# Second layer of a two-block kernel: value tiles loaded between stores, recurrent steps reordered, gate product moved beside the attention

## The chip, the cores and the metric

The kernel runs on one core of one Trainium2 chip. The metric is the device time of one execution in microseconds (us). TensorE (PE) multiplies matrices; VectorE (DVE), ScalarE (ACT) and GpSimd (POOL) do the elementwise work; SyncE (SP) issues nearly all DMA transfers, in the order of its program. Each engine runs its own instructions in order and waits for others on semaphores.

## The reference

A first block (spatial gating, a state space mixer, a router with 16 experts) is followed by a second one, which the change concerns. With 1024 tokens and width 1024:

```python
def hybrid_layer(x, c, ...):
    h = rms_norm_2(x, g_pre) * (1 + scale) + shift
    q, k, v, g_att, u, g_lru, merge = jnp.split(h @ w_in, split_at, axis=-1)
    y_a = (dilated_attention(q, k, v) * jax.nn.silu(g_att)) @ w_pa
    u = causal_depthwise_conv(u, conv_w, conv_b)          # four taps
    y_b = (rg_lru(u, ...) * jax.nn.silu(g_lru)) @ w_pb
    gate_a, gate_b = jnp.split(jax.nn.sigmoid(merge), 2, axis=-1)
    return x + gate * rms_norm_2((gate_a * y_a + gate_b * y_b) @ w_o, g_post)

def rg_lru(u, ...):
    r, i = sigmoid(u @ w_rg + b_rg), sigmoid(u @ w_ig + b_ig)   # block diagonal
    log_a = -LRU_C * r * softplus(-lru_lambda)
    xin = sqrt(-expm1(2 * log_a)) * (i * u)
    h_t = exp(log_a)_t * h_{t-1} + xin_t                        # a scan over the tokens
```

The attention has 12 heads, in three groups of four with dilations 1, 4 and 16.

## The kernel before

Every large product is made in three passes over high and low parts (`three_passes`, L1351 to L1353): an operand is rounded to fp32r on ACT or POOL (the high part), and the rest is subtracted on DVE or POOL (the low part).

**Values.** The second layer starts by turning the normalised tokens and multiplying them with the value weights, 12 tiles of the weight stream (`I_ATT` to `I_PAIR`), in three groups of four tiles. A tile goes into one of four slots of `ring`; SP loads it when PE has finished with the tile before it in the slot, POOL splits it (L1169 high, L1172 low), and PE needs the split tile. Meanwhile ACT scales the eight row tiles of the first layer's result (L2299), and SP stores them (L1022).

**Products in pairs.** All other input products are 30 `PAIRS` p, each made of 7 smaller products i = 0..6 (12 matmuls each, `product(p, i)`), whose sums are put together by ACT (i = 0 at L2359, i = 4 at L2375) and DVE (i = 1, 2, 3, 5, 6 at L3157, L3160, L3175). A product waits for the sums that empty its bank or that it accumulates on: i = 5 for the sum of i = 2, i = 6 for that of i = 3, i = 2 of the next pair for that of i = 5, i = 3 of the next for that of i = 6. The weights of pair p+1 are split by ACT (L2326, at i = 3 to 6 of pair p) and POOL (L1273). A pair that makes gates is followed by `("act", p)`, a Silu or Sigmoid on ACT (L2385), and `("spill", p)`, two stores to DRAM (`gd`).

**The order by hand.** `ORDER2` is one list of events that every engine walks through. In its first part, 84 products (12 pairs), the eight recurrent channels c are woven in: channel c starts behind product `CHANNEL_AT[c]` with `conv` (four taps on DVE, L3184, L3186 twice, L3187, into the one buffer `uc`); three products later comes `gate` (four plain fp32 matmuls of `uc` on PE, L1821; on ACT four sigmoids L2393 and L2395, a Tanh L2400 and an Exp L2401); at +7 `gated` on DVE (L3192, L3194, L3195), at +8 `root` (Sqrt on ACT, L2405), and at +10 `scan` (L3200, L3201), whose result goes to DRAM (`hsd`). The next channel starts at +8 (once at +9).

**Attention units.** Then come six units u of two heads: the pairs Q and K, and a third pair whose products fill the gaps of the attention. For each of eight token tiles tt there are `S` (scores, PE L1831, softmax maximum on DVE), `E` (Exp on ACT, L2411), `PT` (turning, PE L1842, copied by ACT at L2420) and `O` (times V, PE L1854, copied at L2425). With tile 5 and later the first products of the next unit's Q are put in. In the last unit these places hold `B0`, the first half tile of the product of the recurrent branch with `w_pb`. Its operand y is made there: SP reloads the scans and the Silu gates (`yl_raw`, `yl_there`, 16 transfers of 512 KB), POOL multiplies them (L1289), ACT makes the high part (L2429) and DVE the low part (L3222), in the events `("y", c)`.

**The end.** `TURN_ORDER` mixes the rest of the recurrent branch (`B`) with the turning of the combined attention (`OT`, PE L1877), whose three groups DVE combines (L3255 to L3259); then come the other branch (`A`) and the output product.

## Time and profile before

| quantity | value |
|---|---|
| median of 3 runs | 2843.64 us (2843.12 to 2843.66) |
| the profiled execution's own time | 2843.31 us |
| its span in the trace | 2841.5 us |
| TensorE busy | 2736.1 us, 96% of the span |
| VectorE, ScalarE, GpSimd busy | 66%, 53%, 37% |

Terms of the sum are lengths in the profiled execution. Its own time is 1.8 us longer than its span and 0.3 us below the median. The second layer is the part behind about 1700 us. In the rows a time is in us from the span's start; `x8` counts instructions; square brackets hold the idle time of the engine just before and what released it. Starts and lengths of neighbouring matmuls overlap in the record: matmuls of 0.39 us follow each other every 0.23 us.

### The profile page before, as it was taken

What the parts mean: (1) busy time and instruction counts of PE and PEld (TensorE: products, weight loads), DVE (VectorE), ACT (ScalarE), POOL (GpSimd) and SP (SyncE); (2) the same over time, 40 slices, a digit from 0 to 9 for tenths busy, and PEclk for the clock granted to TensorE, in tenths of its full rate; (3) what the DMA queues carried; (4) which work ended last, traced back from release to release, by engine and by line L of the source; (5) the groups of instructions that cost most, each with busy time, mean ns of one, the idle gap of its engine ahead of it and who ended that gap; (6) DMA issues with size and microseconds to landing.
All of it is one profiled execution on the core that took longest, in us unless ns stands there. A gap on an engine that the chain in (4) does not pass through costs nothing.

```text
span 2841.5 us, 35547 instructions
## 1 busy us (share of the span) xinstructions
PE 2736.1 (96%) x12846; PEld 2237.8 (79%) x12846; DVE 1869.3 (66%) x1991; ACT 1495.7 (53%) x1854; POOL 1053.3 (37%) x510
## 2 busy tenths in 40 slices
PE   7999999999999999999999998998899999997999
PEld 6887888478888888888888877986678888886787
DVE  8972114888888888888888887327773233336663
ACT  4231013477777777777777765145564444443021
POOL 0012232013222233333332223567877555555530
PEclk9999999999999999999999999999999999998999
DMA  5021114599999999999999964122222222228441
GB/s 165 30 68 37 38 60 157 236 398 392 383 383 382 383 382 377 388 383 383 382 383 380 379 231 173 54 102 80 86 85 95 84 87 90 76 90 289 142 178 60
DMA packets 162779, 607.41 MB, mean 214 GB/s; under 512 B 20545, under 2 KB 47185, under 8 KB 129649
## 3 DMA queue, kind: packets, MB, share of 16 engines
q1 hardware_dynamic: 156912, 584.84, 54.4%
q0 software_dynamic: 5328, 20.07, 2.5%
q8 instruction: 68, 1.11, 0.2%
q10 hardware_dynamic: 434, 1.08, 0.1%
q14 instruction: 37, 0.30, 0.0%
HBM read 547.11 MB, written 57.78 MB: 213 GB/s over the span
## 4 chain that ended last, share of the span: by engine, by line
PE 81%; DVE 13%; ACT 2%; issue 2%; DMA 1%; POOL 1%; SPq 0%; DVEq 0%; ACTq 0%; POOLq 0%
PE bank L1685 23%; PE bank L1351 17%; PE bank L1353 16%; PE bank L1352 16%; PE bank L1698 2%; PE bank L1821 1%; DVE buffer L3186 1%; PE bank L1831 1%; PE bank L1854 1%; DMA buffer<-gd 1%; POOL buffer L1289 1%; DVE buffer L3187 1%; DVE buffer L3255 1%; PE bank L1842 0%; DVE buffer L3195 0%
## 5 line engine op out<-in xcount | busy, mean ns | idle before, releaser
L2949 DVE TENSOR_TENSOR slots_lo<-buffer,slots_hi 128x2048 fp32r<-128x2048 f32 x383 | 849.2, 2286 | 101.7 <-ACT slots_hi L2194 101.7
L2194 ACT ACTIVATE slots_hi<-buffer 128x2048 fp32r<-128x2048 f32 x384 | 708.8, 1951 | 40.8 <-PE bank L1685 25.4
L1232 POOL DMA_INDIRECT xacc<-buffer x15 | 276.5, 18430 | 615.6 <-ACT buffer L2262 615.6
L1273 POOL TENSOR_TENSOR w_lo_set<-buffer,w_hi 128x512 fp32r<-128x512 f32 x210 | 306.6, 1493 | 155.3 <-ACT w_hi L2326 153.9
L1685 PE MATMUL bank<-slots_hi,xsT_hi 128*128 128x512 f32 x960 | 257.8, 390 | 3.4 <-DVE xsT_lo L2967 3.4
L1685 PE MATMUL bank<-slots_lo,xsT_hi 128*128 128x512 f32 x960 | 257.4, 390 | 0.0
L1685 PE MATMUL bank<-slots_hi,xsT_lo 128*128 128x512 f32 x960 | 257.4, 390 | 0.0
L1685 PEld LDWEIGHTS bank<-slots_hi,xsT_hi 128*128 128x128 f32 x960 | 180.9, 189 | 41.2 <-issue 3.6
L1685 PEld LDWEIGHTS bank<-slots_lo,xsT_hi 128*128 128x128 f32 x960 | 180.8, 188 | 37.7
L1685 PEld LDWEIGHTS bank<-slots_hi,xsT_lo 128*128 128x128 f32 x960 | 180.8, 188 | 37.6
L1351 PE MATMUL bank<-slots_hi,heT_hi 128*128 128x512 f32 x512 | 202.5, 396 | 3.1 <-DVE heT_lo L2999 3.1
L1353 PE MATMUL bank<-slots_hi,heT_lo 128*128 128x512 f32 x512 | 199.6, 390 | 0.0
L1352 PE MATMUL bank<-slots_lo,heT_hi 128*128 128x512 f32 x512 | 199.4, 389 | 0.0
L1351 PE MATMUL bank<-t_hi,w_hi 128*128 128x512 f32 x480 | 194.9, 406 | 0.0
L1353 PE MATMUL bank<-t_hi,w_lo_set 128*128 128x512 f32 x480 | 188.9, 393 | 0.0
L1352 PE MATMUL bank<-t_lo,w_hi 128*128 128x512 f32 x480 | 188.7, 393 | 0.0
L3175 DVE TENSOR_TENSOR buffer<-bank,buffer 128x512 f32<-128x512 f32 x90 | 72.1, 802 | 175.3 <-PE bank L1353 174.6
L2326 ACT ACTIVATE w_hi<-buffer 128x512 fp32r<-128x512 f32 x210 | 120.2, 623 | 100.5 <-POOL buffer L1265 82.8
L1351 PE MATMUL bank<-hT_hi,w_hi 128*128 128x512 f32 x360 | 145.1, 403 | 0.0
L1353 PE MATMUL bank<-hT_hi,w_lo_set 128*128 128x512 f32 x360 | 140.7, 391 | 0.0
L1352 PE MATMUL bank<-hT_lo,w_hi 128*128 128x512 f32 x360 | 140.7, 391 | 0.0
L2021 ACT ACTIVATE buffer<-bank,buffer 128x512 f32<-128x512 f32 x32 | 22.1, 690 | 194.9 <-PE bank L1353 194.9
(538 smaller groups left out, 5661.5 us busy)
## 6 DMA issues: line engine op xcount, KB each, us to landing
buffer<-in_w_gate SPq DMA_DIRECT2D x128, 1024.0 KB, 7.8
buffer<-in_w_up SPq DMA_DIRECT2D x128, 1024.0 KB, 4.8
buffer<-in_w_down SPq DMA_DIRECT2D x128, 1024.0 KB, 7.8
buffer<-in_wstream SPq DMA_DIRECT2D x154, 512.0 KB, 4.2
gd<-buffer SPq DMA_DIRECT2D x28, 512.0 KB, 3.8
buffer<-gd SPq DMA_DIRECT2D x28, 512.0 KB, 7.6
buffer<-in_x SPq DMA_DIRECT2D x16, 512.0 KB, 8.3
od<-buffer SPq DMA_DIRECT2D x48, 130.0 KB, 1.8
```

What stands on the lines that cost most here:

```text
L1232: nc.gpsimd.indirect_dma_start(out=xacc, out_offset=bass.IndirectOffsetOnAxis(ap=idx_scatter, axis=0), in_=ys, in_offset=None, compute_op= ...
L1273: nc.gpsimd.tensor_tensor(lo, chunk_raw[p % 2][i], hi.bitcast(F32), ALU.subtract).then_inc(chunk_split.sem, 1)
L1289: nc.gpsimd.tensor_tensor(yl_raw(c), yl_raw(c), halves(yl_there[:, c]), ALU.mult).then_inc(yl_made.sem, 1)
L1351: mm(bank, lhs[0], rhs[0], start=first, stop=False, skip_group_check=goes_on)
L1352: mm(bank, lhs[0], rhs[1], start=False, stop=False, skip_group_check=goes_on)
L1353: return mm(bank, lhs[1], rhs[0], start=False, stop=last, skip_group_check=goes_on)
L1685: last = mm(psum[first_bank + c][:], x[:, k, :], w_[:, c * HALF:(c + 1) * HALF], start=(k == 0 and x is xsT_hi and w_ is w[0]), stop=(k == ...
L1698: last = mm(psum[4 + c][:], x[:, KD - 1, :], w_[:, c * HALF:(c + 1) * HALF], start=False, stop=x is xsT_lo)
L2194: fn(slots_hi[:, n_ % NH, :], slots[n_ % NS], ACT.Copy).then_inc(slot_high_ready, 1)
L2326: fn(w_hi[n_ % 8], chunk_raw[p % 2][i], ACT.Copy).then_inc(chunk_high.sem, 1)
L2949: tt2(slots_lo[:, place_of(n_), :], slots[n_ % NS], slots_hi[:, n_ % NH, :].bitcast(F32), ALU.subtract).then_inc(slot_split, 1)
L3175: tt2(dst, y_, x_, ALU.add).then_inc(post_done.sem, 1)
```

## The change

Four things, all in the second layer.

1. The loads of value tiles 4 and 5 are issued between the stores of the rows, and tiles 6 and 7 ahead of the first pair's weights.
2. In the recurrent channels the first tap of `conv` goes from DVE to ACT (an Identity with scale and bias, 128x1024), and the square of the decay (L3194) from DVE to ACT. `gate` comes 5 products behind `conv` instead of 3, a new step `mix` (the multiplication of L3192, and ACT's square) at +7, `gated` with what is left of it at +8, `root` at +9, `scan` at +10. Where two fall on one place, the later step of the older channel comes first; before, `conv` did.
3. y is made in 16 pieces of 128x512 during the units: SP loads the scan and the gate (2 x 256 KB), DVE multiplies (`ymul`), SP stores to a new DRAM tensor `yld`. Three pieces fall into each of five units, the last into the sixth. The last unit only loads y. POOL makes the low parts of channels 4 to 7 and DVE those of 0 to 3; `B0` holds two times two channels instead of two times four, and the other four go to the start of `TURN_ORDER`.
4. In the units, one more product of the next Q lies inside the attention, and `act` and `spill` of the fill pair come three products later, so behind the last `E`; in the last unit they come at the very end.

```diff
-CHANNEL_STEPS = (("conv", 0), ("gate", 3), ("gated", 7), ("root", 8), ("scan", 10))
+CHANNEL_STEPS = (("conv", 0), ("gate", 5), ("mix", 7), ("gated", 8), ("root", 9), ("scan", 10))
...
     events = [("prod", p, i)]
-    if i == 0 and p - 1 in GATE_PAIRS:
+    fill = p > N_LRU_PAIRS
+    if i == 3 * fill and p - 1 in GATE_PAIRS:
         events.append(("act", p - 1))
-    if i == 2 and p - 1 in GATE_PAIRS:
+    if i == 2 + 3 * fill and p - 1 in GATE_PAIRS:
         events.append(("spill", p - 1))
+    u, name = (p - N_LRU_PAIRS) // 3, PAIRS[p][0]
+    if name in "QK" or p >= N_LRU_PAIRS:
+        for j, (load, store) in enumerate((((1, 0), (1, 2)), ((1, 4), (1, 6)), ((2, 0), (2, 2)))):
+            if 3 * u + j < 16:
+                if ((p - N_LRU_PAIRS) % 3, i) == load:
+                    events.append(("yload", 3 * u + j))
+                if ((p - N_LRU_PAIRS) % 3, i) == store:
+                    events.append(("ymul", 3 * u + j))
...
-    events += product_events(q, 0) + [("S", u, 0)] + product_events(q, 1) + [("E", u, 0), ("S", u, 1)]
+    events += product_events(q, 0) + [("S", u, 0)] + product_events(q, 1) + [("S", u, 1), ("E", u, 0)]
+    ahead = 2 if last else 3
+    if not last:
+        events += product_events(q, 2)
...
-            events += [("y", c) for c in {1: (4,), 2: (5,), 3: (6, 7), 4: (0, 1), 5: (2, 3)}.get(tt, ())]
+            events += [("y", c) for c in {2: (4,), 3: (5, 6), 4: (7,), 5: (0, 1), 6: (2, 3)}.get(tt, ())]
+    if last:
+        events += [("act", q), ("spill", q)]
...
-TURN_ORDER = [("B", 0, 1), ("B", 1, 0), ("B", 1, 1)]
+TURN_ORDER = [("B", 0, 0), ("B", 0, 1), ("B", 1, 0), ("B", 1, 1)]
...
+                elif kind == "yload":
+                    j = event[1]
+                    c, ts_ = j // 2, slice((j % 2) * HALF, (j % 2 + 1) * HALF)
+                    u = j // 3
+                    hs_stored.wait(sp, 16 * 8)
+                    if j:
+                        y_stored.wait(sp, 16 * j)
+                    for i in range(2):
+                        gates_stored[i].wait(sp, 32 * stores_before(N_LRU_PAIRS + 3 * u + (u + i) % 2))
+                    sp.dma_start(temps[u % 2][:, 1], hsd[c][:, ts_]).then_inc(y_loaded.sem, 16)
+                    sp.dma_start(temps[1 - u % 2][:, 1], gd[GATE_ROW["lg"] + c][:, ts_]).then_inc(y_loaded.sem, 16)
+                elif kind == "ymul":
+                    j = event[1]
+                    yl_made.wait(sp, j + 1)
+                    sp.dma_start(yld[j // 2][:, (j % 2) * HALF:(j % 2 + 1) * HALF], temps[j // 3 % 2][:, 1]).then_inc(
+                        y_stored.sem, 16)
...
-                    fn(ra, ra, ACT.Exp, scale=lru_s[:, c:c + 1]).then_inc(act_to_lru, 1)
+                    fn(ra, ra, ACT.Exp, scale=lru_s[:, c:c + 1]).then_inc(decay_made.sem, 1)
+                elif kind == "mix":
+                    decay_made.wait(act, event[1] + 1)
+                    ii_done.wait(act, event[1] + 1)
+                    fn(uc, ra, ACT.Square).then_inc(act_to_lru, 1)
+                elif kind == "conv":
...
+                    if c:
+                        act.wait_ge(lru_to_act, c)
...
+                    fn(uc, ubufs[c % 2][:, 3:3 + SEQ], ACT.Identity, scale=tap(0, c), bias=col("conv_b", c)).then_inc(
+                        tap_done.sem, 1)
...
-                    step(ts(uc, x[:, 3:3 + SEQ], tap(0, c), col("conv_b", c), ALU.mult, ALU.add))
...
-                    step(tt2(uc, ra, ra, ALU.mult))
                     stt(th, uc, 1.0, th, ALU.add, ALU.mult).then_inc(lru_to_act, 1)
```

SyncE at the first value group, before and then after: `xfd` holds the rows, the single tiles of `in_wstream` at L851 and L865 are value tiles, the twos at L992 and L1006 the first pair's weights.

```order
L988 DMA vd<-buffer 128x512 x4
L1022 DMA xfd<-buffer 128x1024 x8
L992 DMA buffer<-in_wstream 128x1024 x2
L851 DMA buffer<-in_wstream 128x1024 x4
L988 DMA vd<-buffer 128x512 x4
```

```order
L1002 DMA vd<-buffer 128x512 x4
L1035 DMA xfd<-buffer 128x1024 x2
L865 DMA buffer<-in_wstream 128x1024
L1035 DMA xfd<-buffer 128x1024 x2
L865 DMA buffer<-in_wstream 128x1024
L1035 DMA xfd<-buffer 128x1024 x4
L865 DMA buffer<-in_wstream 128x1024 x2
L1006 DMA buffer<-in_wstream 128x1024 x2
```

Two value tiles moved between the rows, and the weights behind all four.

VectorE in the recurrent part, one channel's end and the next one's taps, before (L3192 to L3195 `gated`, L3184 to L3187 `conv`, L3200 and L3201 `scan`) and then after (L3234 `mix`, L3238 `gated`, L3229 and L3230 `conv`, L3244 and L3245 `scan`).

```order
L3192 TENSOR_TENSOR buffer<-buffer 128x1024
L3194 TENSOR_TENSOR buffer<-buffer 128x1024
L3195 SCALAR_TENSOR_TENSOR buffer<-buffer 128x1024
L3175 TENSOR_TENSOR buffer<-bank,buffer 128x512 x2
L3184 TENSOR_SCALAR buffer<-buffer 128x1024
L3186 SCALAR_TENSOR_TENSOR buffer<-buffer 128x1024 x2
L3187 SCALAR_TENSOR_TENSOR buffer<-buffer 128x1024
L3200 TENSOR_TENSOR buffer<-buffer 128x1024
L3201 SCALAR_TENSOR_TENSOR buffer<-buffer 128x1024
```

```order
L3234 TENSOR_TENSOR buffer<-buffer 128x1024
L3203 TENSOR_TENSOR buffer<-bank,buffer 128x512
L3238 SCALAR_TENSOR_TENSOR buffer<-buffer 128x1024
L3229 SCALAR_TENSOR_TENSOR buffer<-buffer 128x1024 x2
L3230 SCALAR_TENSOR_TENSOR buffer<-buffer 128x1024
L3220 TENSOR_TENSOR buffer<-bank,buffer 128x512
L3244 TENSOR_TENSOR buffer<-buffer 128x1024
L3245 SCALAR_TENSOR_TENSOR buffer<-buffer 128x1024
```

Two instructions of the chain left VectorE, and a sum (L3203) stands between the pieces of the older channel.

ScalarE near the end of an attention unit, before (L2385 the fill pair's activation, L2411 `E`, L2425 and L2420 the copies of `O` and `PT`) and then after (L2416, L2457, L2471, L2466).

```order
L2385 ACT_TABLE_LOAD
L2385 ACTIVATE buffer<-buffer 128x2x512 x2
L2425 ACTIVATE buffer<-bank 128x256
L2420 ACTIVATE buffer<-bank 128x256
L2411 ACT_TABLE_LOAD
L2411 ACTIVATE buffer<-buffer 128x128 x2
```

```order
L2457 ACTIVATE buffer<-buffer 128x128 x2
L2471 ACTIVATE buffer<-bank 128x256
L2466 ACTIVATE buffer<-bank 128x256
L2357 ACTIVATE w_hi<-buffer 128x512 x2
L2416 ACT_TABLE_LOAD
L2416 ACTIVATE buffer<-buffer 128x2x512 x2
L2471 ACTIVATE buffer<-bank 128x256
```

The activation, and with it both switches of the table, moved from between two `E` to behind the last `PT`.

## Rows read from the trace of the kernel before

**Rows 1.** The page: busy time, share of the span and instructions of each engine.
```profile
PE 2736.1 (96%) x12846; PEld 2237.8 (79%) x12846; DVE 1869.3 (66%) x1991; ACT 1495.7 (53%) x1854; POOL 1053.3 (37%) x510
```

**Rows 2.** PE's waits, 1700 to 2842: waiting, releaser, us in total, times, longest.
```profile
PE bank L1821 <- DVE buffer L3187: 22.4, 7, 4.7
PE bank L1854 <- ACT buffer L2420: 19.5, 10, 8.2
PE bank L1351 <- POOL ring_lo L1172: 10.1, 1, 10.1
PE bank L1842 <- ACT buffer L2411: 8.8, 6, 1.7
```

**Rows 3.** Chain of waits, 1725 to 1765: start, length, what.
```profile
1734.74 8.33 ACT buffer L2299 x8
...
1746.33 6.60 DMA buffer<-in_wstream
...
1752.98 3.17 POOL ring_hi L1169
...
1756.22 4.27 POOL ring_lo L1172
```

**Rows 4.** Timeline of PE, and windows: PE, PEld, DVE, ACT, POOL busy, clock, DMA.
```profile
1760.54 0.81 PE L1351 MATMUL bank<-ring_hi,hT_hi 128*128 128x512 f32 x1 [10.12 <-POOL ring_lo L1172]
...
1760.00:1765.00 5.00, 4.46 (x13) 3.84 (x14) 4.96 (x2) 1.91 (x1) 4.92 (x3) 0.62 0.42 140
...
1895.00:2135.00 240.00, 217.57 (x854) 162.77 (x854) 172.88 (x117) 141.05 (x181) 188.47 (x100) 0.96 0.22 83
2150.00:2550.00 400.00, 388.80 (x1911) 327.58 (x1910) 127.22 (x203) 174.89 (x409) 232.80 (x184) 0.99 0.25 85
2555.00:2612.00 57.00, 39.70 (x188) 32.47 (x187) 38.38 (x38) 25.21 (x61) 38.18 (x17) 0.85 0.81 287
```

**Rows 5.** Timeline of PE in the recurrent part: gate matmuls without and with a wait.
```profile
1900.49 3.59 PE L1821 MATMUL bank<-buffer 128*128 128x512 f32 x8
...
1988.52 5.40 PE L1821 MATMUL bank<-buffer 128*128 128x512 f32 x8 [4.62 <-DVE buffer L3187]
```

**Rows 6.** Timelines of DVE and ACT in the recurrent part.
```profile
1870.77 0.69 DVE L3175 TENSOR_TENSOR buffer<-bank,buffer 128x512 f32<-128x512 f32 x1 [4.68 <-PE bank L1353]
1873.49 0.69 DVE L3175 TENSOR_TENSOR buffer<-bank,buffer 128x512 f32<-128x512 f32 x1 [2.03 <-PE bank L1353]
...
1895.17 2.61 DVE L3186 SCALAR_TENSOR_TENSOR buffer<-buffer 128x1024 f32<-128x1024 f32 x2
...
2005.68 1.58 DVE L3192 TENSOR_TENSOR buffer<-buffer 128x1024 f32<-128x1024 f32 x1
2007.30 2.20 DVE L3194 TENSOR_TENSOR buffer<-buffer 128x1024 f32<-128x1024 f32 x1
...
2021.45 3.24 DVE L3201 TENSOR_TENSOR_SCAN buffer<-buffer 128x1024 f32<-128x1024 f32 x1
...
1905.34 1.15 ACT L2400 ACTIVATE buffer<-buffer 128x1024 f32<-128x1024 f32 x1
```

**Rows 7.** Timeline of ACT late in unit 4, and what PE waited for there.
```profile
2514.55 1.28 ACT L2385 ACT_TABLE_LOAD   x1
2515.85 2.01 ACT L2385 ACTIVATE buffer<-buffer 128x1024 f32<-128x1024 f32 x2
...
2520.64 0.44 PE L1842 MATMUL bank<-buffer 128*128 128x128 f32 x2 [1.48 <-ACT buffer L2411]
```

**Rows 8.** Timelines of POOL, ACT and PE in the last unit.
```profile
2574.16 2.34 POOL L1289 TENSOR_TENSOR buffer<-buffer 128x1024 f32<-128x1024 f32 x1 [16.25 <-DMA buffer<-gd]
...
2576.53 1.06 ACT L2429 ACTIVATE yl_hi<-buffer 128x1024 fp32r<-128x1024 f32 x1 [6.24 <-POOL buffer L1289]
...
2600.18 1.22 PE L1854 MATMUL bank<-buffer 128*128 128x128 f32 x4 [8.20 <-ACT buffer L2420]
```

**Rows 9.** The page's DMA issues: how many, KB each, median us to landing.
```profile
gd<-buffer SPq DMA_DIRECT2D x28, 512.0 KB, 3.8
buffer<-gd SPq DMA_DIRECT2D x28, 512.0 KB, 7.6
```

122 lines of the change are left out of this document (66 added, 56 removed).

## Prediction

> **What bounds the kernel now.** I read the page first: TensorE is busy 96% of the span [rows 1], so nothing but its 4% of pauses, and the stretches at the lower clock, can be won; no matmul is added or removed. Then its table of waits in the second layer [rows 2]. The four longest make 60.8 us, and the change goes for all of them: the gate matmuls wait 22.4 us for the last tap of the convolution, the attention's O waits 19.5 us and its PT 8.8 us for ScalarE, and the second value group waits 10.1 us for one split weight tile. Third, the windows, for what the clock takes on top [rows 4]: in 1895 to 2135 the granted clock is 0.96 of full, so 240 x 0.04 = 9.6 us more; in 1760 to 1765 it is 0.62, 5 x 0.38 = 1.9 us; in 2150 to 2550 it is 0.99, 4 us. The two levels are 2.4 and 1.2 GHz, and the same eight gate matmuls take 3.59 us without a wait and 5.40 us behind one of 4.62 us [rows 5]: a pause of about 4 us costs 1.8 us again. So some 61 us of waits and 16 us of clock are there to be had, and the question is how much of it the new order gives back.
>
> **Value tiles.** PE's wait is 10.12 us [rows 4], so group 0 ended at 1760.54 - 10.12 = 1750.4. The chain is ScalarE's eight row tiles, 8.33 us from 1734.74 (1.04 each), the stores and the weights in SP's order, the tile's load landing 6.60 us after its issue (1746.33), and 3.17 + 4.27 us of GpSimd [rows 3]. After the change the load goes out behind the second row, at about 1734.7 + 2 x 1.04 + 1 of issue + 1 for the load = 1738.8; it lands by 1745.4 with the same 6.6 us and is split by 1752.8 with the same contended 7.4 us. But VectorE is what GpSimd shares that time with, and it starts its joins only when all rows are stored (it did at 1748.3, between the load and the split); so most of the split meets an idle VectorE. With less traffic ahead, I take 1750 and no wait, and 1750.4 to 1755.3 as the range (landing 9 us, full contention). The gain is 10.1 + 1.9 = **12.0 us**, at worst 7. Two loads among the rows delay the last row by about 2.7 us, hence the joins; the first pair needs them some 60 us later, which covers that. Nothing else moves: tiles 5 to 7 are there sooner than PE, at 11 us a tile, wants them.
>
> **Recurrent channels.** Unit of time: one product, 2.72 us (two sums that each follow a product stand 2.72 us apart, 0.69 us long) [rows 6]. A 128x1024 step on VectorE costs 1.3 us alone (2.61 for two) and 2.20 us beside GpSimd [rows 6]. GpSimd is busy 188 of 240 us here [rows 4], so I take 2.2 for taps and `gated`, 1.6 for the multiplication, 1.15 for a 1024-wide ACT step, and 1.6 + 3.24 for `scan`. Let 0 be the end of the product at +6, so `mix` comes first. VectorE: a sum to 0.7, `mix` to 2.3. ScalarE squares to 3.4. VectorE: sum of the next product (ends at 2.7) to 3.5, `gated` to 5.7. ScalarE's tap to 6.9. VectorE's three taps to 13.5. The gate now stands behind five further products, at 6 x 2.72 = 16.3, so **its wait is gone** (22.4 us). What is late next: the sums of those products, which stand in VectorE's queue behind the taps. PE runs into them where product i = 5 or 6 comes three behind an unsummed one, or i = 2 or 3 four behind.
>
> Place by place, with i the first product behind `conv`. Channel 1 (i = 1): ScalarE has a Silu in the way (a table load 1.28 and 2.01 [rows 7]), the tap ends at 8.5, the taps at 15.2, the sums of i = 1 and 2 at 16.6; i = 5 wanted them at 13.6: stop 3.0. Channel 2 (i = 2): taps 13.6, sum 14.3, i = 5 wanted it at 10.9: 3.4. Channel 3 (i = 3): a Silu between Exp and square, sum at 15.2, wanted at 10.9: 4.3. Channel 4 (i = 4): none. Channel 5: 0.7. Channel 6: none. Channel 7 (i = 1, with a Sigmoid): 3.0. Together **14.4 us of new stops**, on PE's product waits instead of its gate waits. The scan behind the taps (4.8 us, to about 20) meets the gate and its 3 us on PE, and costs nothing as long as the taps are no later. Clock: four stops of 3 to 4.3 us against five of 3.5 to 4.7 us, 6.6 against 9.6 us. Result 32.0 - 21.0 = **11 us**. Bounds: taps at 1.3 us (GpSimd idle) shorten every stop by 2.7 us, leaving 2.9 us and no clock loss, a gain of 29; each of the four stops 2 us longer (a ScalarE that is late with the tap) leaves a gain of 1. I take the contended end, since the steps of rows 6 in mid channel are at 2.20.
>
> A table switch shows as 1.28 us, and the activation starts right behind it, 2515.85 after 2514.55 [rows 7]. The Trainium skill, "ScalarE: Activation LUTs", section "What ACT_TABLE_LOAD costs", adds a drain of 1.38 us to each switch. This trace has no such gap at that row. By the page three of the stops would be 1.4 us longer and the sum 4 us smaller. Another rule speaks against steps beside GpSimd. The rows show 2.20 us beside it against 1.3 us alone for one shape [rows 6]. "SBUF — State Buffer" in the Trainium skill, section "SBUF: two separate sides", calls the port that both share an exclusive lock: a step waits out a whole GpSimd instruction, then runs at full speed. By that, with 2.34 us of GpSimd [rows 8] ahead of every tap, three taps would take 10.9 us, and the first rival below would be the outcome; no step of these rows is that long, so it adds little to that rival's chance.
>
> **Attention units.** The activation of the fill pair takes 1.28 + 2.01 us, and then Exp's own table 1.28 us, all between two E's; PT waits 1.48 us behind it in unit 4 [rows 7]. The five units carry 11.2 of the 28.3 us of [rows 2] (the window 2150 to 2550 has 400 - 388.8 us idle [rows 4]) and 4 us of clock. Now both switches stand behind the last PT. What waits for them: O's copy, which nothing on PE needs, and the next unit's first E, which has two products, 5.4 us, above it for a softmax of about 1 us, a table of 1.28 and the Exp. So **15 us**, at worst 9 if the new DVE multiplications hold up the softmax. Those are 16 steps of about 0.7 to 1.2 us on an engine busy 127 of 400 us [rows 4], with 768 KB each of traffic in a window with the DMA queues at a quarter. Their loads have two products of 2.72 us to land. Where they are late, VectorE stands up to 2 us with two sums queued behind, inside the 5.4 us that those have. SP stands in front of each store; queued behind it are O's stores, the value loads (three tiles ahead) and, once per unit, none of the pair weights, which are issued first.
>
> **Last unit.** PE idles 57 - 39.7 = 17.3 us in 2555 to 2612 [rows 4], mostly in 4.6 and 8.2 us where ScalarE's copy of PT stands behind a high part that waits for GpSimd, which waits for reads of 512 KB, 16 of them in all (idle 16.25 us, then 2.34 us and 1.06 us each) [rows 8]. About 6.8 us of matmuls run at the low clock there, 2.5 us lost. After: eight of the sixteen 512 KB reads and all multiplications are gone, the high parts start behind tile 2, with four products (15 us) above the load. But tiles 5 to 7 have no product between PT and O, only 1.4 us of B0: there each copy waits for 2 x 1.06 us of high parts. I count 0.5 + 0.8 + 1.0 + 0.7 + 1.2 us for PT and O of these tiles, and 1.0 us where the low parts of channels 2 and 3 come late: 5.2 us, and a clock drop at most. The activation at the very end holds SP's statistics back by 1.28 + 2.01 us and two stores; 2.7 us of B that moved behind O cover it. So 17.3 + 2.5 - 5.2 - 1.8, rounded down for that tail: **12 us**, 5 to 17.
>
> **Sum.** 12 + 11 + 15 + 12 = 50 us. The profiled execution took 2843.3 us, so 2793.3; the median of the runs is 0.3 us above it. Forecast **2793 us**. Half of the forecast's uncertainty is the recurrent part.
>
> **Rivals.**
> - *VectorE's debt eats the recurrent gain.* Stops at sums as long as the old gate waits: the other three parts alone, 2843 - 39 = 2804. For it: VectorE's chain per channel loses only 2 steps of about 3 us, and ScalarE gets two more with waits in its queue; against it: the gate's slack is 13.6 us instead of 8.2.
> - *Everything hides.* With two steps fewer, GpSimd and VectorE meet less, taps near 1.3 us: recurrent 29 instead of 11, last unit 17: 2843 - 73 = 2770.
> - *The value tile isn't earlier.* Traffic of the rows delays the load as before, and 7 to 12 us stay: about 2802.
> - *Slower: SP blocks.* Each piece of y is a round trip in SP's queue: 7.6 us for the read, 0.7 for the step and 3.8 us for the store [rows 9] make 12 us against 5.4 us of cover, and if it reached PE each time, 16 x 6.7 = 107 us, 2843 - 50 + 107 = 2900. It turns the sign from 3.1 us per piece on. Against it: those landings are of 512 KB, the pieces are half, and the queues are idle then.
>
> **How the numbers follow.** Forecast 0.5, VectorE's debt 0.2, value tile 0.08, everything hides 0.17, slower 0.03, and 0.02 for no change. The range 2776 to 2812 takes in the forecast with its bounds and the first and third rival, and leaves out most of "everything hides" and the slow one. A difference of 0.2% (5.7 us) is what a measurement of this kernel tells from none. Faster 0.95, same 0.02, slower 0.03.
>
> **What would show it.** PE's wait for `ring_lo` gone; waits for L3187's successor small, and new ones of 3 to 4 us at L1351 on a DVE sum, in channels 1, 2, 3 and 7; the PT waits of units 0 to 4 gone; in the last unit waits of about 1 us at tiles 5 to 7. Wrong would be: a gate wait above 2 us, a wait on `w_lo_set` (GpSimd or ScalarE late with weights), or waits on VectorE's multiplication of y.

## The result and the profile after

The changed kernel takes **2791.3 us** (median of four runs, 2789.5 to 2793.9) against 2843.4 us before (median of four, 2839.1 to 2843.7). The ratio is 0.982, with a 95% interval of 0.980 to 0.984. The forecast was 2793 us. Its profiled execution took 2791.3 us, with a span of 2789.5 us.

To see where the 52.0 us between the two spans went, I cut both traces at the same five events of the program. Each row below is the time from one event to the next, read from the timelines; the code of the first and the last stretch is unchanged.

| stretch | before | after | saved | forecast |
|---|---|---|---|---|
| start to the first product of the value group 0 (1697.64, 1694.44) | 1697.6 | 1694.4 | 3.2 | 0 |
| values: to the first sum of pair 0 (1859.89, 1844.70) | 162.2 | 150.3 | 12.0 | 12 |
| recurrent: to S(0,0) (2184.94, 2162.52) | 325.1 | 317.8 | 7.2 | 11 |
| units: to S(5,0) (2558.37, 2517.82) | 373.4 | 355.3 | 18.1 | 15 |
| last unit: to the first OT (2628.83, 2576.78) | 70.5 | 59.0 | 11.5 | 12 |
| from there to the end | 212.7 | 212.7 | 0.0 | 0 |

The first row is no work of the change. Over the kernels of this study, all with the same code up to that point, that event stands anywhere from 1693.8 to 1698.5 us. That is why the experiments below are read by stretch and not by their total. How far a stretch repeats where its code is the same has to be known too. The value stretch (150.3 us) and the units (355.3) agree within 0.1 us. The recurrent stretch took 317.2 to 317.8 us in four kernels and 315.1 in two, a difference that lies in TensorE's clock (more at the end). The last unit took 58.7 to 60.5 us in nine. So a difference under some 3 us in the recurrent stretch, or under 2 us in the last unit, says little by itself, and the 7.2 us of the third row could as well have been some 10.

The page of the changed kernel, its line of busy times (it answers to [rows 1]: the same 12,846 matmuls, 17 us less of them):

```profile
PE 2719.2 (97%) x12846; PEld 2232.7 (80%) x12846; DVE 1842.3 (66%) x1987; ACT 1511.7 (54%) x1869; POOL 1027.9 (37%) x506
```

PE's waits in the changed kernel, 1700 to 2842 (columns as in [rows 2]):

```profile
PE bank L1383 <- DVE buffer L3203: 9.1, 3, 3.8
PE bank L1383 <- DVE buffer L3220: 7.1, 2, 4.5
PE bank L1886 <- issue: 4.9, 1, 4.9
...
PE bank L1886 <- ACT buffer L2466: 1.8, 2, 1.0
...
PE bank L1874 <- ACT buffer L2457: 1.2, 2, 0.9
```

The four waits of [rows 2] are gone or much smaller. The gate matmuls (L1853 now) don't appear, `ring_lo` doesn't, PT (L1874) has 1.2 us left of 8.8 and O (L1886) 6.7 of 19.5, of which 4.9 are a new wait in the last unit. In their place stand L1383 on VectorE's sums L3203 and L3220, 16.2 us: products that wait for a bank or an addend.

The windows show what the clock did. First the changed kernel, the recurrent stretch, the units, the last unit; then the same three of the kernel before (columns: window, its length, busy time of PE, PEld, DVE, ACT, POOL, granted clock, DMA share, GB/s):

```profile
1844.70:2162.52 317.82, 300.44 (x1228) 235.27 (x1227) 161.77 (x130) 187.66 (x244) 246.96 (x154) 0.97 0.26 93
...
2162.52:2517.82 355.30, 355.30 (x1794) 302.28 (x1793) 140.94 (x209) 166.06 (x395) 212.55 (x165) 1.00 0.36 121
2517.82:2576.78 58.96, 51.04 (x249) 42.29 (x248) 35.11 (x60) 26.52 (x64) 22.37 (x10) 0.94 0.85 275
```

```profile
1859.89:2184.94 325.05, 302.62 (x1228) 232.92 (x1227) 195.29 (x144) 171.23 (x229) 260.44 (x154) 0.97 0.24 88
...
2184.94:2558.37 373.43, 362.23 (x1794) 305.60 (x1793) 122.81 (x195) 167.59 (x396) 209.86 (x165) 0.99 0.25 85
2558.37:2628.83 70.46, 53.16 (x249) 43.61 (x248) 47.91 (x64) 25.87 (x63) 35.28 (x14) 0.88 0.83 288
```

The difference between length and PE's busy time is idle time; the difference in busy time, at the same number of matmuls, is the clock. Units: 11.2 us of idle time and 6.9 us of clock are gone, and TensorE has no gap left. Recurrent: idle 22.4 to 17.4 us, clock 2.2 us. Last unit: idle 17.3 to 7.9 us, clock 2.1 us.

**The value tile.** SP's queue and GpSimd in the changed kernel:

```profile
1734.01 0.46 SPq L865 DMA_DIRECT2D buffer<-in_wstream  x1
```
```profile
1738.90 1.04 POOL L1204 CAST ring_hi<-buffer 128x1024 fp32r<-128x1024 f32 x1 [11.24 <-DMA buffer<-in_wstream]
1740.03 2.38 POOL L1207 TENSOR_TENSOR ring_lo<-buffer,ring_hi 128x1024 fp32r<-128x1024 f32 x1
```

The load is issued behind the stores of the first two rows, which SP began at 1732.60, and is there 4.9 us later; GpSimd splits it in 1.04 + 2.38 us, where it took 3.17 + 4.27 us beside VectorE's joins [rows 3]. Tile 4 is ready at 1742.4, PE begins with it at about 1747.2, and has no wait.

**The new stops.** Timeline of PE in the recurrent stretch of the changed kernel, four of the six waits over 0.2 us:

```profile
1941.51 0.50 PE L1383 MATMUL bank<-hT_hi,w_hi 128*128 128x512 f32 x1 [2.71 <-DVE buffer L3203]
...
2022.07 0.50 PE L1383 MATMUL bank<-hT_hi,w_hi 128*128 128x512 f32 x1 [1.18 <-ACT buffer L2406]
...
2032.31 0.79 PE L1383 MATMUL bank<-t_hi,w_hi 128*128 128x512 f32 x1 [4.48 <-DVE buffer L3220]
...
2092.06 0.62 PE L1383 MATMUL bank<-hT_hi,w_hi 128*128 128x512 f32 x1 [3.82 <-DVE buffer L3203]
```

These are channel 2, channel 5 (two) and channel 7; channel 1 has one of 2.59 us at 1915.99 and channel 3 one of 2.61 us at 1971.28, on VectorE's sums too. Together they are 17.4 us. The forecast had 3.0, 3.4, 4.3, 0.7 and 3.0 us there. All but the 1.18 us are at sums behind the taps as forecast, but channel 5 has 5.7 us instead of 0.7. The rows there, from SP, DVE, POOL and ACT in the changed kernel:

```profile
2005.67 0.33 SPq L1127 DMA_DIRECT2D hsd<-buffer  x1
2006.04 1.74 SPq L1006 DMA_DIRECT2D buffer<-in_wstream  x2
```
```profile
2002.38 3.26 DVE L3245 TENSOR_TENSOR_SCAN buffer<-buffer 128x1024 f32<-128x1024 f32 x1
...
2021.57 2.03 DVE L3238 SCALAR_TENSOR_TENSOR buffer<-buffer 128x1024 f32<-128x1024 f32 x1 [6.90 <-ACT buffer L2436]
```
```profile
2013.53 2.29 POOL L1297 TENSOR_TENSOR buffer<-buffer 128x512 f32<-128x512 f32 x1 [6.82 <-DMA buffer<-in_wstream]
```
```profile
2019.96 0.63 ACT L2357 ACTIVATE w_hi<-buffer 128x512 fp32r<-128x512 f32 x1 [5.22 <-POOL buffer L1300]
2020.50 1.04 ACT L2436 ACTIVATE buffer<-buffer 128x1024 f32<-128x1024 f32 x1
```

Read from the top: SP waits for the end of channel 3's scan (2002.38 + 3.26), stores it, and only then loads the weights of pair 8. GpSimd's sums for that pair wait 6.8 us for the load; ScalarE's high part waits 5.2 us for GpSimd; the square of channel 4 stands behind that high part in ScalarE's queue; `gated` of channel 4 (L3238) waits 6.9 us for the square, and behind it stand channel 5's taps and the sums that PE wants. Five queues in a row, each in order. The load is 7.6 us late: the product that frees the weights' place had ended at 1998.4.

**The last unit.** SP's queue and PE in the changed kernel:

```profile
2542.72 8.54 SPq L1030 DMA_DIRECT2D buffer<-od  x5
...
2552.01 0.55 SPq L1019 DMA_DIRECT2D buffer<-vd  x1
```
```profile
2554.80 1.19 PE L1886 MATMUL bank<-buffer 128*128 128x128 f32 x4 [4.88 <-issue]
```

The five loads of the attention's statistics take SP 8.5 us to issue; the last value tile's load stands behind them and O of tile 7 wants that tile. Before the change PE's waits for ScalarE [rows 8] held it past this load.

### The profile page after: what moved, and what is told of

It reads as the page before. It is cut to its first block, busy times and chain, and to the rows that moved or that the text cites. A ratio compares the mean times of both kernels' runs of the same rounds, so it can differ in the third digit from the quotient of the medians.

```text
span 2789.5 us, 35655 instructions
## 1 busy us (share of the span) xinstructions
PE 2719.2 (97%) x12846; PEld 2232.7 (80%) x12846; DVE 1842.3 (66%) x1987; ACT 1511.7 (54%) x1869; POOL 1027.9 (37%) x506
## 4 chain that ended last, share of the span: by engine, by line
PE 83%; DVE 11%; ACT 2%; issue 2%; POOL 1%; DMA 1%; SPq 0%; DVEq 0%; ACTq 0%; POOLq 0%
PE bank L1717 23%; PE bank L1383 17%; PE bank L1385 17%; PE bank L1384 17%; PE bank L1730 2%; PE bank L1886 1%; PE bank L1863 1%; DVE buffer L3229 1%; PE bank L1853 1%; DVE buffer L3304 1%; PE bank L1874 1%; PE bank L1780 0%; DVE buffer L3230 0%; PE bank L1739 0%; DVE heT_lo L3045 0%
## 5 line engine op out<-in xcount | busy, mean ns | idle before, releaser
L1383 PE MATMUL bank<-slots_hi,heT_hi 128*128 128x512 f32 x512 | 202.4, 395 | 3.1 <-DVE heT_lo L3045 3.1
L1383 PE MATMUL bank<-t_hi,w_hi 128*128 128x512 f32 x480 | 195.6, 408 | 7.1 <-DVE buffer L3220 7.1
L3220 DVE TENSOR_TENSOR buffer<-bank,buffer 128x512 f32<-128x512 f32 x90 | 71.9, 802 | 163.3 <-PE bank L1385 162.7
L1383 PE MATMUL bank<-hT_hi,w_hi 128*128 128x512 f32 x360 | 146.1, 406 | 10.3 <-DVE buffer L3203 9.1
```

Of the source, the lines that this page charges most:

```text
L1383: mm(bank, lhs[0], rhs[0], start=first, stop=False, skip_group_check=goes_on)
L3220: tt2(dst, y_, x_, ALU.add).then_inc(post_done.sem, 1)
```

## Experiments

Theory: the value, unit and last-unit gains are each their own part's; the recurrent gain is the gate's new place less the sums that the taps hold up; channel 5's excess comes from SP's order. Line numbers differ a little from kernel to kernel; the operations are the same. Each kernel below was run once, apart from the last two.

### The value tiles in the old order

```diff
             store_values(0, 0)
-            store_rows(0)
-            store_rows(1)
-            load_tile(I_ATT + 4)
-            store_rows(2)
...
+            for tt in range(NT):
+                store_rows(tt)
+            load_weights(0)
+            for i in range(I_ATT + 4, I_ATT + 8):
+                load_tile(i)
```

> The changed kernel with SP's old order of the value tiles (all eight rows stored, weights of pair 0, then tiles 4 to 7). Theory: the value part of the gain is the position of one load; TensorE waits about 10 us for the split tile 4 again and pays 1.9 us at the lower clock behind it, the stretch up to the first pair's first sum grows by 12 us, the rest stays, about 2803 us. Rival: the tile is late for GpSimd's and VectorE's shared work rather than for its position; then a wait of under 5 us comes back, under 2797 us.

2801.6 us. The value stretch takes 161.2 us, 10.9 more than in the changed kernel, and the other stretches are what they were (317.4, 355.3, 59.2). PE waits again:

```profile
1754.33 0.81 PE L1377 MATMUL bank<-ring_hi,hT_hi 128*128 128x512 f32 x1 [7.82 <-POOL ring_lo L1201]
```

The wait is 7.8 us and not 10.1, since this time the load landed in 5.9 us and not 6.6, and GpSimd's high part took 1.52 us and not 3.17. So the order of these loads and stores in SP's queue gives 10.9 of the 12.0 us.

### The gate three products behind the convolution again

```diff
-(("conv", 0), ("gate", 5), ("mix", 7), ("gated", 8), ("root", 9), ("scan", 10))
+(("conv", 0), ("gate", 3), ("mix", 7), ("gated", 8), ("root", 9), ("scan", 10))
```

> The changed kernel with the gate matmuls three products behind the convolution, as before, and all else new. Theory: the stops of the changed kernel (17.4 us on product waits, at sums that stand behind the taps in VectorE's queue) and the gate waits of before are one debt: with the gate at +3 it waits for the last tap some 2 to 3 us in each of 7 or 8 channels (15 to 22 us), and the product stops shrink to under 5 us, since TensorE's pause lets VectorE catch up; about 2793 to 2800 us. Rival: the stops have another cause (ScalarE or GpSimd late by themselves); then they stay at 17 us and the gate waits come on top, 2810 us or more.

2800.6 us; the recurrent stretch takes 322.1 us, 4.3 more. PE's waits over 0.2 us in it are now these alone:

```profile
PE bank L1853 <- DVE buffer L3230: 20.0, 6, 4.4
```

The product stops are gone altogether, and 20.0 us stand at the gates instead of 17.4 at the products. So the stops are the same debt in another place, as the theory has it: VectorE needs the time for the taps, and PE pays for it where it first wants something. The gate's new place alone is worth 4.3 us, with the 2.7 us by which the changed kernel's own recurrent stretch varies still to be kept in mind.

### Tap 0 and the square on VectorE again

```diff
                 elif kind == "conv":
...
+                    step(ts(uc, x[:, 3:3 + SEQ], tap(0, c), col("conv_b", c), ALU.mult, ALU.add))
...
                 elif kind == "gated":
...
+                    step(tt2(uc, ra, ra, ALU.mult))
```

> The changed kernel with the first tap and the square back on VectorE, in the new order of steps. Theory: VectorE's queue is what ends last in a channel; two steps of 2.2 us more and 1 to 1.7 us of hand-over less make the taps end about 2 to 3 us later, each of the five stops at sums (channels 1, 2, 3, 5, 7) grows by that and some gate waits of 1 to 2 us appear, 10 to 20 us more, 2801 to 2811 us. Rival: ScalarE's late tap and square are what holds the chain; then the time stays at 2791 or falls.

2793.4 us, and the recurrent stretch takes 317.6 us, 0.2 less. The expected 10 to 20 us did not come; the rival is closer. With both steps back on VectorE (168.9 instead of 138.8 us busy in 1880 to 2115) the kernel is 0.2 us faster there than the changed kernel, and 2.5 us slower than the two kernels that have the changed kernel's recurrent code and took 315.1 us. The waits (PE, 1700 to 2842):

```profile
PE bank L1383 <- DVE buffer L3188: 11.2, 3, 5.2
...
PE bank L1383 <- DVE buffer L3205: 4.6, 1, 4.6
PE bank L1383 <- POOL w_lo_set L1308: 3.7, 1, 3.7
```

Channels 2 and 3 do stop longer (5.2 and 4.6 us against 2.7 and 2.6), as expected, but channel 5's 5.7 us is not at a sum at all any more: there PE waits 3.7 us for split weights, which are late for the same weight load (GpSimd's sums waited 10.7 us for it). Moving steps to ScalarE had put the square behind a high part that waits for GpSimd; of the 4.5 us that the sums gained in channels 2 and 3, 1.9 were lost at channel 5 and 0.5 at channel 7. All stops together are 19.5 us against 17.4. That the stretch is no longer comes from PE's busy time, 298.1 us against 300.4, and such a difference shows between kernels of the same code too. So here the two steps on ScalarE are worth something between nothing and 2.5 us.

### The activation at its old place in the units

```diff
-    fill = p > N_LRU_PAIRS
+    fill = 0
```

> The changed kernel with a fill pair's activation and its store at their old places in the next pair (behind its products 0 and 2), all else new. Theory: PT waits behind the activation and its table loads as before, the five units S(0,0) to S(5,0) take 15 to 18 us longer, about 2807 to 2809 us. Rival: the gain of the units came from the order of E and S and the third product ahead, which stay; then under 5 us come back, about 2795 us.

2803.2 us. The units take 366.3 us, 11.0 more: 7.3 us of idle time and 3.7 us of clock. PE waits in each of the five units, the longest 1.5 us (the line counts three short waits of the last unit too, and leaves out three of O in the units, 1.3 us together):

```profile
PE bank L1874 <- ACT buffer L2457: 7.6, 8, 1.5
```

That is between the theory's 15 to 18 and the rival's 5. So part of the 18.1 us belongs to the order of the units, or to both together, which the next kernel tells.

### The old order of the units with the activation at its new place

```diff
-    events += product_events(q, 0) + [("S", u, 0)] + product_events(q, 1) + [("S", u, 1), ("E", u, 0)]
-    ahead = 2 if last else 3
-    if not last:
-        events += product_events(q, 2)
+    events += product_events(q, 0) + [("S", u, 0)] + product_events(q, 1)
+    events += [("S", u, 1), ("E", u, 0)] if last else [("E", u, 0), ("S", u, 1)]
+    ahead = 2
```

> The changed kernel with the first five units in the old order of products, S and E (two fill products ahead instead of three, E of tile 0 ahead of S of tile 1), while the activation keeps its new place. With the activation alone put back the five units had lost 11.0 of the 18.1 us they gained. Theory: the two parts add, the old order costs the other 7 us, 2798 us. Rival: they overlap, since both act on the same wait of PT for ScalarE, and the order alone is worth under 2 us once no activation stands there, 2791 to 2793 us; then with both undone more is lost than the sum of each.

2791.5 us; the units take 355.8 us, 0.5 more, with one wait of 0.53 us in them. The rival is right: alone, the order is worth 0.5 us. Undone alone, the parts cost 11.0 and 0.5 us. With both undone, in the kernel before, the cost is 18.1, so 6.6 us are had by either of them. (The kernel before also lacks the pieces of y, which cost the units nothing, as the next experiment shows.) A likely reason, not followed through the traces, is that both parts give ScalarE's Exp and copy more time before PT and O want them.

### y handled as before

```diff
+            def multiply(c):
+
+                hs_loaded[c // 4].wait(pool, 64)
+                sl_loaded[c // 4].wait(pool, 64)
+                nc.gpsimd.tensor_tensor(yl_raw(c), yl_raw(c), halves(yl_there[:, c]), ALU.mult).then_inc(yl_made.sem, 1)
...
-                elif kind == "yload":
...
-                elif kind == "ymul":
```

> The changed kernel with y handled as before: read, multiplied on GpSimd and split in the last unit, with the activation behind tile 5 there, and no pieces of y in the units. Theory: the last unit, S(5,0) to the first OT, takes about 70 us again instead of 59 (waits for the copies of PT behind high parts that wait for GpSimd), the units before it lose nothing, so 2801 to 2804 us. Rival 1: the pieces of y cost the units something; then the five units get shorter than the 317.8 us from first sum to S(0,0) and 355.3 us from S(0,0) to S(5,0) of the changed kernel, by up to 3 us. Rival 2: the last unit's gain came from its own order and not from y; then it stays near 60 us.

2805.9 us. The last unit takes 72.6 us, 13.7 more, and the units 355.3 us, as with the pieces. In the last unit PE waits as before [rows 2]:

```profile
PE bank L1873 <- ACT buffer L2454: 16.7, 5, 8.2
```

The first rival fell: the 16 pieces of y cost the units nothing. The gain of the last unit goes with y, but this kernel also has the old places of `B0` and of the activation in the last unit, so what those two give by themselves is not shown. DMA share in the units rose from 0.25 to 0.36 without a wait.

### The weights of pair 8 ahead of channel 3's store

```diff
                             load_weights(p + 2)
+                            if p == 6:
+                                scanned.wait(sp, 4)
+                                sp.dma_start(hsd[3], th).then_inc(hs_stored.sem, 16)
...
-                elif kind == "scan":
+                elif kind == "scan" and event[1] != 3:
```

> The changed kernel with one change in SP's order: the weights of pair 8 are loaded ahead of the store of channel 3's scan, not behind it. Theory: the stops in channel 5 (1.18 + 4.48 us) start there. In the changed kernel SP waits until the scan's end at 2005.67 us and only then issues the load, GpSimd's sums wait 6.8 us for it, ScalarE's high part for GpSimd, and the square of channel 4, the `gated` step and channel 5's tap stand behind that. With the load first both stops go, 5 to 6 us and the clock behind them, 2785 us. Rival: VectorE is late there anyway (as the first forecast had it, 0.7 us at least); then a stop of 2 to 4 us stays and the time is 2788 us or more.

2786.0 us; the recurrent stretch takes 311.0 us, 6.8 less than in the changed kernel. Not all of it is the load's: by the end of product 49, before the moved load can act, this kernel is 1.6 us ahead already (152.1 us from the first sum for 153.7), at the same stops and a higher clock. The two kernels with the old load and the same head start took 315.1 us, so the load gives 4.1 us, 2.9 of them in stops. SP and PE in it:

```profile
1998.77 0.80 SPq L1006 DMA_DIRECT2D buffer<-in_wstream  x2
2006.74 0.33 SPq L1075 DMA_DIRECT2D hsd<-buffer  x1
```
```profile
2028.31 0.50 PE L1386 MATMUL bank<-t_hi,w_hi 128*128 128x512 f32 x1 [1.65 <-DVE buffer L3223]
```

Channel 5 stops for 1.65 us instead of 1.18 + 4.48, between the theory's nothing and the rival's 2 us, and channel 7 for 4.85 instead of 3.82. The five stops are now 2.6, 2.7, 2.6, 1.65 and 4.85 us, 14.4 together. That this is the forecast's sum to the tenth is luck, since the single stops differ from it by up to 1.9 us; but the excess of channel 5 was this one load in SP's queue.

### The high parts of pair 9 behind the square of channel 5

```diff
-                    for j in W_HIGH_AT.get(i, ()) if p + 1 < N_PAIRS else ():
+                    for j in W_HIGH_AT.get(i, ()) if p + 1 < N_PAIRS and (p, i) not in ((8, 3), (8, 4)) else ():
...
                     fn(uc, ra, ACT.Square).then_inc(act_to_lru, 1)
+                    for j in range(4) if event[1] == 5 else ():
+                        chunk_high_part(9, j)
```

> The changed kernel with ScalarE's square of channel 5 ahead of the four high parts of the next pair's weights, which wait there for GpSimd's sums and those for a weight load. Theory: the 4.48 us stop of channel 5 comes from ScalarE standing 5.2 us at such a high part with the square queued behind; with the square first it starts 2 to 3 us earlier, and the stops of channel 5 (1.18 + 4.48 us) shrink by 2 to 4 us, 2788 us. Rival: VectorE's own queue is late there; then they stay, and the later high parts may even cost a wait for split weights.

2796.4 us; the two stops are unchanged (1.18 and 4.47 us), and channel 7's rose from 3.82 to 6.08 us.

This experiment missed its mark. The square that is late before channel 5's taps is that of channel 4, and the high part ahead of it belongs to pair 8; the edit moved those of pair 9. It says nothing on channel 5. At channel 7 it shows the same link. A high part of ScalarE stands there for GpSimd's sums 12.2 us (10.1 in the changed kernel), the square of channel 6 behind it comes 2.2 us later, and the taps and sums of channel 7 behind that: 2.3 us more at the stop and 2.8 us in the stretch.

### VectorE's taps one product apart

```diff
-(("conv", 0), ("gate", 5), ("mix", 7), ("gated", 8), ("root", 9), ("scan", 10))
+(("conv", 0), ("tapb", 1), ("tapc", 2), ("gate", 5), ("mix", 7), ("gated", 8), ("root", 9), ("scan", 11))
...
                     x = ubufs[c % 2]
-                    for i in (1, 2):
-                        step(stt(uc, x[:, 3 - i:3 - i + SEQ], tap(i, c), uc, ALU.mult, ALU.add))
+                    step(stt(uc, x[:, 2:2 + SEQ], tap(1, c), uc, ALU.mult, ALU.add))
+                elif kind == "tapb":
+                    c = event[1]
+                    x = ubufs[c % 2]
+                    step(stt(uc, x[:, 1:1 + SEQ], tap(2, c), uc, ALU.mult, ALU.add))
+                elif kind == "tapc":
+                    c = event[1]
+                    x = ubufs[c % 2]
                     stt(uc, x[:, 0:SEQ], tap(3, c), uc, ALU.mult, ALU.add).then_inc(uc_ready, 1)
```

> The changed kernel with VectorE's three taps one product apart, so that each product's sum stands between two taps (channel 3's three stay together, since the next sum overwrites their input), and the scan one product later. Theory: the stops are sums queued behind three taps in a row; with at most one tap ahead of a sum those of channels 1, 2, 5 and 7 shrink from 12.9 us (2.59 + 2.71 + 1.18 + 4.48 + 3.82 less 1.9 left at the late chunk of channel 5) to under 3 us, channel 3 keeps 2.6, gate waits of up to 1 us may come in three or four channels; 8 to 12 us less, 2780 to 2784 us. Rival: VectorE is short of time as such (taps plus sums longer than the products they stand beside); then the same microseconds come back as gate waits or at later products, 2789 to 2793 us.

**2776.0 us**, more than expected. The recurrent stretch takes 299.8 us, 18.0 less than in the changed kernel. DVE in channel 2, where the changed kernel had stopped for 2.7 us:

```profile
1933.23 2.11 DVE L3229 SCALAR_TENSOR_TENSOR buffer<-buffer 128x1024 f32<-128x1024 f32 x1 [1.49 <-ACT buffer L2447]
1935.38 0.69 DVE L3204 TENSOR_TENSOR buffer<-bank,buffer 128x512 f32<-128x512 f32 x1
1936.11 1.48 DVE L3233 SCALAR_TENSOR_TENSOR buffer<-buffer 128x1024 f32<-128x1024 f32 x1
1937.62 0.69 DVE L3221 TENSOR_TENSOR buffer<-bank,buffer 128x512 f32<-128x512 f32 x1
1938.23 1.60 DVE L3237 SCALAR_TENSOR_TENSOR buffer<-buffer 128x1024 f32<-128x1024 f32 x1
```

A tap, a sum, a tap, a sum, a tap: the sums leave at 1935.4 and 1937.6, where the changed kernel had them behind all three taps. No product waits any more in channels 1, 2, 5 and 7. Of PE's waits over 0.2 us in the stretch two are left, one of 1.3 us at a gate and one of 4.9 us at a sum of channel 3.

Of 17.4 us of stops 6.3 are left, and the rest of the 18.0 us is the clock: PE is busy 293.6 us for the 300.4 before, at 0.99 in place of 0.97. Not all of it is the taps'. With the scan one product later SP also issues pair 8's weights ahead of channel 3's store, as in the experiment before last; against that kernel's 311.0 us the stretch is 11.2 us shorter, and this is what the taps one product apart give, together with the later scan, which was not tried alone. The other 6.8 us are the load's 4.1 and the clock's 2.7. The 4.9 us of channel 3, whose three taps stay together, is longer than the 2.6 us it was. There VectorE's sum, with all else behind it, had waited for ScalarE's copy of the product's first quarter, which stands behind the gate's six steps and Exp's table in ScalarE's queue:

```profile
1952.59 0.69 DVE L3201 TENSOR_TENSOR buffer<-bank,buffer 128x512 f32<-128x512 f32 x1 [6.06 <-ACT buffer L2391]
```

So ScalarE is what is late next.

### The statistics behind the last value load

```diff
-                        for u in range(UNITS - 1):
-                            load_stats(u // 2, u % 2)
...
                     if n + 3 < NT * UNITS:
                         load_value(n + 3)
+                    if n + 4 == NT * UNITS:
+                        for u in range(UNITS - 1):
+                            load_stats(u // 2, u % 2)
```

> The changed kernel with the five loads of the attention's statistics on SP behind the last value load instead of ahead of it. Theory: the wait of 4.88 us at O of tile 7 in the last unit is for the value tile whose load stands behind those five in SP's queue (8.5 us of issue); it goes, and the last unit is 4 to 5 us shorter, with a clock drop less, about 2786 us; the statistics are not wanted before VectorE merges the layers. Rival: the wait is ScalarE's copy of PT behind its high parts; then it stays at 3 to 5 us and the time at 2791.

2786.7 us; the last unit takes 56.3 us, 2.7 less. PE in it, and the value load in SP's queue:

```profile
2549.21 0.68 PE L1887 MATMUL bank<-buffer 128*128 128x128 f32 x4 [1.59 <-issue]
...
2554.62 0.50 PE L1384 MATMUL bank<-yl_hi,late_hi 128*128 128x512 f32 x1 [2.35 <-DVE yl_lo L3272]
```
```profile
2540.85 0.48 SPq L1019 DMA_DIRECT2D buffer<-vd  x1
2541.37 8.90 SPq L1030 DMA_DIRECT2D buffer<-od  x5
```

Counted from S(5,0) the load goes out 8.8 us earlier, and the wait of 4.88 us falls to 1.59, so it was SP's queue and not ScalarE. But a new wait of 2.35 us follows for VectorE's low parts of y, so PE's idle time in the last unit falls by 0.9 us only, from 7.9 to 7.0. The other 1.8 us are clock: 49.2 us busy for 51.0, and the granted clock is 1.00 in place of 0.94. The two kernels below have this order too and took 58.1 and 56.5 us, against the 58.7 to 60.5 of the nine with the old one.

### Both improvements, and both with the two steps on VectorE

> Both improvements in one kernel: VectorE's taps one product apart with the scan one product later, and the statistics loads behind the last value load. Theory: they lie in different stages and add; the recurrent stretch takes 300 us instead of 318, the last unit 56 to 57 instead of 59, about 2773 us, 0.975 of the kernel before. Rival: in the last unit the new wait for VectorE's low parts of y takes the second part back, 2776 us.

The kernel with the taps apart and the statistics moved takes **2773.0 us** (five runs, 2770.1 to 2773.8), a ratio to the kernel before of 0.976 [0.974, 0.977]. That is 18 us under the changed kernel. The recurrent stretch is 299.9 us, as with the taps alone, with the same stop of 4.9 us. The last unit is 58.1 us, more than the expected 56 to 57; PE waits 2.2 us for the low parts of y in it.

The second kernel differs from it in tap 0 and the square alone, which are VectorE's again, by the edit shown above.

> The kernel with both improvements, but first tap and square of each channel on VectorE again. Theory: now that sums stand between the taps VectorE's own time decides; per channel it has some 23 us of steps and sums in the 25 us that eight products and a gate take, against 19 us with the two steps on ScalarE, so gate waits or stops of 1 to 2 us appear in most channels, 8 to 16 us more than the kernel with both on ScalarE, 2781 to 2789 us. Rival: as in the changed kernel, where putting them back cost nothing, the hand-overs to ScalarE cost what the steps save; then 2773 us.

2779.8 us (four runs, 2778.8 to 2781.6; 0.978 [0.977, 0.980]), 6.8 us more. The recurrent stretch takes 306.5 us, 6.6 more, under the expected 8 to 16 but far from the rival's nothing. In the changed kernel the same edit had cost 2.5 us at most. So ScalarE's share is worth 6.6 us in this order, in which the sums no longer stand behind three taps and the weight load no longer behind a scan. Without it PE stops for 5.8 us at channel 3's sum (4.9 before), for 1.8 us at channel 2's and for 2.4 us at a gate (1.2 before).

## Why the prediction was right

**The total** came out 1.7 us under the forecast, but the profiled execution owes 3.2 us to the first stretch, which no edit touches. By the stretches that the change does touch it saved 48.8 us where 50 were forecast. Part of that closeness is luck: the recurrent part gave 3.8 us less than forecast, the units 3.1 more.

**Values**: 12.0 us, as forecast. The mechanism held, with faster steps than taken: 4.9 us of landing and 3.4 us of split, where the forecast took 6.6 and 7.4. The tile was ready 4.8 us before PE came to it, where the sum had it 2.4 us late by its own terms and then took no wait. The rival that the load would be delayed by the rows fell.

**Recurrent**: 7.2 us for 11, the term with the widest bounds. The gate waits went entirely, as forecast, and stops came at sums in the channels named. Three of them were shorter than forecast (2.6, 2.7, 2.6 for 3.0, 3.4, 4.3), and the taps took 2.06 us in the median, so the contended 2.2 us was the right end to take. Channel 7's was longer (3.8 for 3.0). The step that failed is "channel 5: 0.7". It went through PE's and VectorE's queues alone. It did not look at SP's, where the store of channel 3's scan stands ahead of pair 8's weights, nor at ScalarE's, where the square now stands behind a high part that waits for those weights. The order in SP's queue is not new. The kernel before had the same load even later, 9.3 us behind the product that frees its place (it ended at 2015.7, when PE began to wait for channel 4's gate):

```profile
2024.71 0.33 SPq L1092 DMA_DIRECT2D hsd<-buffer  x1
2025.08 1.26 SPq L992 DMA_DIRECT2D buffer<-in_wstream  x2
```
```profile
2031.15 1.29 POOL L1262 TENSOR_TENSOR buffer<-buffer 128x512 f32<-128x512 f32 x1 [5.36 <-DMA buffer<-in_wstream]
```

There PE had stopped 3.5 us at the gate, ScalarE's high part waited only 0.9 us for GpSimd, and the square was a step of VectorE's own. The change took that cover away and put the square behind the high part. The experiment on that load gives 4.1 us back, and leaves 14.4 us of stops. The clock's part was sized too high: 6.6 us were forecast for 14.4 us of stops, where PE's busy time with 14.4 us of stops is only 3.1 us above that with 6.3. The changed kernel lost more, since its clock fell more often than in others with its code (300.4 us busy against 297.9). "ScalarE's two steps help" was a silent part of the same term; in this order of work they gave 2.5 us at most.

**Units**: 18.1 us for 15. The waits of 11.2 us went as forecast; the clock's term was mis-sized. I took 4 us from a mean clock of 0.99 over 400 us, a figure with two digits. The busy time of the same matmuls shows 362.2 against 355.3 us, so 6.9 us. The rival that SP or VectorE block on pieces of y fell: PE did not wait once.

**Last unit**: 11.5 us for 12, partly by luck. Idle time fell by 9.4 us where 12.1 were forecast, and the clock gave 2.1 us where 0.7 were. The forecast's 2.5 us for the clock of before does not follow from its 6.8 us of matmuls at half the clock, which lose 3.4; by busy time it is 4.0 us, 53.2 for the 49.2 at a clock of 1.00. Forecast were 5.2 us of small waits at tiles 5 to 7 and late low parts; the small ones at tiles 5 to 7 came to 2.7 us (1.03 + 0.76 + 0.87), and 4.9 us stood at a place that I had not named: the last value load behind five statistics loads in SP's queue. The old wait for ScalarE had covered it.

**The rivals**: VectorE's debt was real in kind (20.0 us at the gates when they stand at +3, 17.4 us at the products now), but the longer slack did buy 4.3 us. "Everything hides" was wrong for this order, and its time was nearly right for the one with the taps apart, 2776 us for its 2770, but not by its mechanism: there too taps beside GpSimd take up to 2.2 us.

## What to carry to other kernels

When a change removes a wait, look for what that wait had covered, in every queue, the one that only issues DMAs too. Both surprises here were loads that stood behind a store or behind other loads in SP's order before the change as well. Uncovered they cost some 4 and 2 us. Where one engine does long steps for a later consumer and short ones for an early one, interleave them: putting each product's sum between two taps, with the same instructions, gave some 11 us where moving two of the long steps to another engine had given 2.5 us at most. And read a change by stretches between fixed events of the program, with busy time and idle time apart.

## What the runs showed of the hardware

**The clock's part of a pause shows in busy time.** In the recurrent stretch the same matmuls took 302.6 us with 22.4 us of pauses, 300.4 with 17.4, 296.6 with 14.4 and 293.6 with 6.3. So removing 16 us of pauses gave 9 us more on top, for stops of 1 to 5 us each, with the granted clock going from 0.97 to 0.99 of its full level. It is not a fixed price: kernels with the same code and the same six stops took 317.2 to 317.8 us in four cases and 315.1 us in two, and what differs is again PE's busy time, 300.4 in the changed kernel against 297.9 here (the kernel with the statistics moved, window of the same stretch):

```profile
1845.15:2160.21 315.06, 297.86 (x1229) 233.39 (x1227) 161.84 (x130) 187.40 (x244) 247.67 (x154) 0.98 0.26 94
```

The difference can be followed to single stops. Behind channel 3's stop of 2.6 us the clock fell to 1.2 GHz in the changed kernel and stayed at 2.4 GHz in the other, in the same 3.3 us of the same code (first the changed kernel, whose mean of 0.56 and 10 matmuls stand against 1.00 and 16):

```profile
1972.40:1975.70 3.30, 3.30 (x10) 2.56 (x9) 3.27 (x2) 0.00 (x0) 3.30 (x2) 0.56 0.00 0
```
```profile
1972.85:1976.15 3.30, 3.30 (x16) 2.75 (x15) 3.27 (x2) 0.00 (x0) 3.30 (x2) 1.00 0.02 5
```

That is 1.7 us; the other 1.0 us comes at channel 5's stops. So a stop of 2.6 us costs sometimes more than itself and sometimes not, and why is not shown.

**VectorE and GpSimd side by side.** GpSimd's split of a value tile took 1.04 + 2.38 us with VectorE idle, and 3.17 + 4.27 us beside its joins [rows 3]. One line's instructions in the changed kernel, the taps and GpSimd's low parts (shortest, median and longest in ns):

```profile
L3229 DVE SCALAR_TENSOR_TENSOR buffer<-buffer x16: 1283/2058/2207, 1879.5 to 2086.2; 128x1024 f32<-128x1024 f32 x16
```
```profile
L1308 POOL TENSOR_TENSOR w_lo_set<-buffer,w_hi x210: 1267/1297/3275, 1799.8 to 2516.1; 128x512 fp32r<-128x512 f32 x105
```
The Trainium skill, "SBUF — State Buffer", section "SBUF: two separate sides", has the two take turns for whole instructions. Taking turns, a tap and such a subtraction would need 1.28 + 1.30 = 2.6 us each round; the longest tap took 2.2 us, so some of the work overlaps here, and the loss is smaller than by the page. A longer stretch says the same. From 2020.0 to 2032.7 GpSimd did seven subtractions without a pause:

```profile
2020.00 12.65 POOL L1308 TENSOR_TENSOR w_lo_set<-buffer,w_hi 128x512 fp32r<-128x512 f32 x7
```

Beside them VectorE did `gated` and three taps. By the shortest record of each kind (1.27 us for a subtraction, 1.23 for `gated`, 1.28 for a tap) those eleven instructions need 8.9 and 5.1 us, 14.0 together, and 12.65 were enough.

**Table loads.** In the recurrent stretch of the changed kernel, as in [rows 7], an activation starts as soon as the 1.28 us of its table load are over: Sqrt's load is at 1995.05 us, its activation at 1996.34. The drain of 1.38 us that the Trainium skill, "ScalarE: Activation LUTs", section "What ACT_TABLE_LOAD costs", adds did not show between them in the rows read, and the stops that it would have made longer came out shorter than forecast.
